# Another order of the steps in the three attention loops of a two-block kernel: scores, outputs, transposes, other work

## The reference

```python
for l in range(2):
    x  = ffn(x);  xc = ffn(xc)
    u  = mod_norm(x) @ w_in[l];  uc = mod_norm(xc) @ w_in[l]
    if l == 0:      # the context tokens are used as keys alone in the last layer
        yc = concat(conv(uc), pool(uc), softmax(qc kc' / 8) vc) @ w_out[l]
        xc = ffn(xc + gate * yc)
    # latent queries in blocks of 128: 8 rows x 16 columns; their keys are a band of
    # 32 columns in each of 8 rows (256 keys, bias from a table, masked) and 256 context keys
    y = concat(conv(u), pool(u), softmax([q k_near' / 8 + bias, q kc' / 8]) [v_near, vc]) @ w_out[l]
    x = ffn(x + gate * y)
```

## Time and profile before

| | |
|---|---|
| time, median of 3 runs | 3379.51 us (3378.93 to 3380.56) |
| profiled execution | 3378.85 us, of which the span of the trace is 3377.0 us |
| TensorE (matmuls) busy | 3265.8 us, 97% |
| VectorE busy | 2493.1 us, 74% |
| ScalarE busy | 1275.4 us, 38% |
| context loop in the trace | 1438 to 1503.4 us |
| first latent loop | 1548.3 to 1643.3 us |
| second latent loop | 2837.1 to about 2960 us |

### The profile page before, as it was taken

How to read it: one execution, slowest core, us unless ns; L and a number is a source line. 1 busy time by engine, 2 the same in 40 slices (tenths; PEclk the granted TensorE clock), 3 DMA queues, 4 the chain that set the end, 5 groups by cost and what they waited for, 6 DMA issues and landing times. The chain is left out here.

```text
span 3377.0 us, 45852 instructions
## 1 busy us (share of the span) xinstructions
PE 3265.8 (97%) x18042; PEld 2901.4 (86%) x18042; DVE 2493.1 (74%) x4610; ACT 1275.4 (38%) x2257; POOL 628.6 (19%) x657
## 2 busy tenths in 40 slices
PE   7989999999999999999999999999999999999998
PEld 6788778888999998978899999989999978788887
DVE  5576578888888997576788889888999865653333
ACT  4475542333323234334533333443332343432222
POOL 0100011112422220301052222142222212000000
PEclk9999999999999999999999999999999999999999
DMA  5201245564233333522113333323333343123332
GB/s 168 63 26 51 80 159 184 172 187 135 74 110 118 117 91 113 149 88 81 60 57 111 117 113 106 97 72 103 103 111 118 94 128 87 38 81 98 96 99 77
DMA packets 381929, 348.90 MB, mean 103 GB/s; under 512 B 17440, under 2 KB 338336, under 8 KB 381200
## 3 DMA queue, kind: packets, MB, share of 16 engines
q1 hardware_dynamic: 337696, 250.74, 24.5%
q0 software_dynamic: 17232, 46.84, 4.7%
q10 hardware_dynamic: 26784, 48.37, 4.6%
HBM read 339.60 MB, written 2.10 MB: 101 GB/s over the span
## 5 line engine op out<-in xcount | busy, mean ns | idle before, releaser
L816 PE MATMUL ps<-Hh,hib 128*128 128x512 f32 (+2 forms) x2672 | 956.2, 358 | 14.2 <-DVE Hl L2508 6.4
L816 PE MATMUL ps<-Hl,hib 128*128 128x512 f32 (+2 forms) x2672 | 947.0, 354 | 0.0
L816 PE MATMUL ps<-Hh,lob 128*128 128x512 f32 (+2 forms) x2672 | 946.4, 354 | 0.0
L1604 ACT ACTIVATE hib<-rawb 128x1024 fp32r<-128x1024 f32 (+2 forms) x589 | 508.3, 872 | 573.6 <-PE ps L816 570.7
L2376 DVE TENSOR_TENSOR lob<-rawb,hib 128x1024 fp32r<-128x1024 f32 (+2 forms) x361 | 441.0, 1225 | 384.6 <-ACT hib L1604 382.5
L816 PEld LDWEIGHTS ps<-Hh,hib 128*128 128x128 f32 x2672 | 507.9, 190 | 77.9 <-DVE Hl L2508 12.1
L816 PEld LDWEIGHTS ps<-Hh,lob 128*128 128x128 f32 x2672 | 507.8, 190 | 52.6
L816 PEld LDWEIGHTS ps<-Hl,hib 128*128 128x128 f32 x2672 | 508.4, 190 | 49.2 <-issue 0.5
L816 PE MATMUL ps<-Gha,hib 128*128 128x512 f32 (+1 forms) x704 | 238.6, 339 | 4.8 <-DVE lob L2376 3.4
L816 PE MATMUL ps<-Gla,hib 128*128 128x512 f32 (+1 forms) x704 | 237.3, 337 | 0.0
L816 PE MATMUL ps<-Gha,lob 128*128 128x512 f32 (+1 forms) x704 | 236.6, 336 | 0.0
(11 more groups left out here) (329 smaller groups left out, 5863.8 us busy)
## 6 DMA issues: line engine op xcount, KB each, us to landing
rawb<-in_ffn_w_in SPq DMA_DIRECT2D x114, 512.0 KB, 3.8
rawb<-in_ffn_w_out SPq DMA_DIRECT2D x76, 512.0 KB, 3.4
rawb<-in_w_in SPq DMA_DIRECT2D x74, 512.0 KB, 3.7
rawb<-in_w_ff SPq DMA_DIRECT2D x64, 512.0 KB, 3.6
rawb<-in_ffn_w_in SPq DMA_DIRECT2D x124, 256.0 KB, 3.3
MRa<-in_w_mod_t ACTq DMA_DIRECT2D x117, 256.0 KB, 3.1
MR<-in_w_mod_t POOLq DMA_DIRECT2D x112, 256.0 KB, 3.4
MRb<-in_w_mod_t ACTq DMA_DIRECT2D x59, 256.0 KB, 3.1
```

The source lines that it names most:

```text
L816: return e.matmul(out, lhsT, rhs, start=start, stop=stop)
L1604: return e.activation(out, src, f, **k)
```

## The change

TensorE's order in the latent and context loops goes from *transposes(step-d), scores(step), other work, outputs(step-d), bank of outputs(step-d-1) back* to *scores(step), outputs(step-d-1), their bank back at once, transposes(step-d), other work*, with d = `depth(s)`. The outputs of a pair are so issued one step later than before. ScalarE's order goes from *copies of the transposes(step-d), exponentials(step), other work, high half of the outputs(step-d-1)* to *high half of the outputs(step-d-1), copies(step-d), exponentials(step), other work*. VectorE's order stays. The number of steps, which was taken from the last entry of the skew list, is now an argument with the same value. No instruction is added or taken away.

```diff
-def by_pairs(number, stages, skew, beside, beside_do):
+def by_pairs(number, stages, skew, beside, beside_do, last):
 
-    for step in range(number + skew[-1]):
+    for step in range(number + last):
...
 (TensorE)
-                by_pairs(len(pairs), [n_turn, n_scores, "beside", n_out, n_final],
-                         [depth(s), 0, 0, depth(s), depth(s) + 1], beside_pairs(l, s), beside_do)
+                by_pairs(len(pairs), [n_scores, n_out, n_final, n_turn, "beside"],
+                         [0, depth(s) + 1, depth(s) + 1, depth(s), 0], beside_pairs(l, s), beside_do, depth(s) + 1)
...
 (ScalarE)
-                by_pairs(len(pairs), [n_turn, n_scores, "beside", n_final], [depth(s), 0, 0, depth(s) + 1], beside_pairs(l, s), beside_do)
+                by_pairs(len(pairs), [n_final, n_turn, n_scores, "beside"], [depth(s) + 1, depth(s), 0, 0], beside_pairs(l, s), beside_do,
+                         depth(s) + 1)
...
 (VectorE)
-                by_pairs(len(pairs), [n_scores, n_scale, "beside", n_final], [0, 1, 0, depth(s) + 1], beside_pairs(l, s), beside_do)
+                by_pairs(len(pairs), [n_scores, n_scale, "beside", n_final], [0, 1, 0, depth(s) + 1], beside_pairs(l, s), beside_do,
+                         depth(s) + 1)
```

## The result

| | before | after |
|---|---|---|
| time, median of 4 runs | 3380.03 us (3378.93 to 3380.56) | 3397.64 us (3395.78 to 3401.09) |
| span of the profiled execution | 3377.0 us | 3394.9 us |
| context loop, first scores to last outputs | 64.53 us | 74.06 us |
| first latent loop | 93.47 us | 95.85 us |
| second latent loop | 121.55 us | 127.78 us |

The change makes the kernel slower: by 17.6 us between the medians, which is 0.52%; the ratio on record is 1.0059 (95% interval 1.0046 to 1.0072). The loops' lengths are read on TensorE's timeline, from the start of the first row of scores to the start of the last row of outputs. They grew by 9.53 + 2.38 + 6.23 = 18.1 us, where the span grew by 17.9. The two other differences are −3.3 us ahead of the context loop and +3.0 between the latent loops, where both kernels issue the same instructions (more on this at the end).

A forecast was written before the change was run, and what follows sets the result against it. TensorE, busy 97% of the span, was taken to bound the kernel. Added waits of 8.7 (context), 2.5 (first latent) and 5.5 us (second latent) plus 6.8 for the clock gave 23.5, so 3403 us, range 3388 to 3414.

The forecast's parts named there:

- Transposes(2) for final(0): Context loop, step 4: transposes wait for VectorE's `n_final` of step 0, which frees the outputs' bank; +0.9 us.
- Outputs(3) for final(2): Context loop, step 6: outputs wait for VectorE's `n_final` of step 2, where nobody waited before; +1.4 us.
- Scores(7) for final(3): Context loop, step 7: scores wait 7.2 us for VectorE's `n_final` of step 3, behind convolution stage 1; +6.4 us.
- Scores(11) for exponentials(10): First latent loop, where tiles end: scores wait 2.1 us for a bank ScalarE's exponentials free, before 0.29; +1.8 us.
- Edge waits: First latent loop, steps with a tile: banks come free about when a 7.0 us step needs them; 0.3 us in all.
- Scores(9): Second latent loop: scores wait 4.3 us for VectorE's `n_final` of step 4, where it was 0.85; +3.4 us.
- The start: Second latent loop: transposes(0) instead of scores(3) wait for exponentials(2), saving 0.7 of the 2.67 us wait.
- The clock: TensorE's clock drops behind waits: 2.4 us each for two long ones, 1.0 each for two of 2.1; +6.8 us.
- The rule of the Trainium skill: Rival: short frequent waits in tile-less latent steps make TensorE alternate to half clock; some +15 us, 3418; 4 in 100.
- 1.84 did nothing: Argument against the half-clock rival: around the second latent loop's 1.84 us wait the clock stayed at 1.00.
- no work is added: Step in the sum: the change adds no work, and dense products behind the loops take nothing back.
- The faster rival: If VectorE's `n_final` of steps 3 and 4 is never waited for: up to 7.6 us gained, 3372 to 3377; 6 in 100.

The follow-up runs named there:

- experiment 1: Kernel before, with TensorE's and ScalarE's new order in the context loop only, old order in both latent loops: 3389.51 us, ratio 1.0033.
- experiment 2: Changed kernel with ScalarE's old order, so only TensorE's order is new: 3399.34 us, ratio 1.0062.
- experiment 4: Changed kernel, but in layer 0 (context and first latent loop) the outputs' bank returns to the list a step later: 3399.13 us, ratio 1.0059.
- experiment 5: Changed kernel with VectorE's `n_final` (low half of the outputs) ahead of its "beside" work: 3371.29 us, ratio 0.9981.
- experiment 8: New order with VectorE's early low half, and on ScalarE exponentials ahead of the copies: 3381.02 us, ratio 1.0010.
- experiment 3: Changed kernel with TensorE's old order, so only ScalarE's order is new: 3378.37 us, ratio 1.0001.
- experiment 6: Kernel before, with only VectorE's low half of the outputs moved ahead of its other work: 3381.33 us, ratio 1.0009.
- experiment 7: New order with VectorE's early low half in the context and second latent loops, first latent loop as before: 3372.68 us, ratio 0.9985.

## Why the prediction came out

The sign, the place and the releaser of each main wait came out as predicted, but for the start of the second latent loop; the time was 5 to 6 us too high, by a term that the sum lacked. Of the signs listed, one was just missed: the long wait was to be 6 to 8 us and was 5.94. Two small readings in the sum were off without consequence: final(4) ended at 2904.81 and not 2904.73, and 2903.7 less 2899.5 is 4.2, not 4.3.

**Waits.** Sums of TensorE's waits in the three loops, from its timeline:

| | before | after | more | predicted |
|---|---|---|---|---|
| context loop | 2.81 us | 10.41 us | +7.6 | +8.7 |
| first latent loop | 3.87 | 6.18 | +2.3 | +2.5 |
| second latent loop | 5.96 | 12.17 | +6.2 | +5.5 |

- *Context loop.* Transposes(2) for final(0): 1.43 in place of 0.52, +0.9 as predicted. Outputs(3) for final(2): 1.57, predicted 1.4. Scores(7) for final(3): 5.94, predicted 7.2; where the clock held ahead of it, in experiments 1 and 2, 7.40 and 7.39. From the low half's start to the end of final(3) were 10.21 us (1484.91 to 1495.12), predicted 10.2. Experiments 4 (bank's turn) and 5 (VectorE's order) remove these waits in different ways, which confirms the mechanism.
- *First latent loop.* Scores(11) for exponentials(10): 1.72, predicted 2.1. Edge waits: 0.51 in one place, 0.3 charged. Drain: 0.78, 0.78, 0.69 and 0.69 in place of 1.18, 0.69 and 0.69, the +0.4 predicted.
- *Second latent loop.* Outputs(2): 1.34, predicted 1.5. Scores(9): 3.80, predicted 4.3. Scores(13) and (15): 1.72 and 1.74, predicted 2.1 and 1.65. The start was wrong: instead of 2.0 in one wait there came 1.59, 0.64 and 0.56, together 2.8, so no part of the 2.67 was saved.

**The clock.** Predicted +6.8, measured +6.6, but by errors that cancel. From the windows, stretches at half clock with work under them: 1.7 us behind 1481, 1.9 behind the long wait, 1.7 behind 1617.86, 3.0 behind 2913.11, 1.7 behind 2942.10, together 10.0; and before 3.4 at the start of the second latent loop that are gone (the 1.7 at the start of the first are in both). I had charged 2.4 for each of the two long waits and 1.0 for each of the two of 2.1; the drop behind 1481 and the one saved at 2853 were in no term. The long wait's own stretch of half clock was 6.8 us long (1492 to 1500, at 0.54 and 0.61) and cost 1.9, since nearly half of it lay under the wait itself. The rule of the Trainium skill ("TensorE: Matmul & The Clock Gate", A second HAM failure mode) that I had made a rival did not come true here: in the steps without a tile, where it should have shown, the window from 1622 to 1626 is at 1.00, and each latent loop has one drop there, of 1.7 us, behind its wait of 1.72. In experiment 8, where four such steps in a row wait 0.5 to 0.6 us, the clock is 1.00 from 1602 to 1640. The argument held against that rival, "1.84 did nothing", was luck, though: in experiments 1, 3 and 6 a drop came behind the same wait of 1.84 us.

**The missing term.** Waits +16.1 and clock +6.6 give 22.7, and the loops got 18.1 longer. The 4.6 us between are in the steps that nothing holds up. I had taken a step's length as 6.97 in either order, as if only the waits could differ. The changed kernel shows (timeline of TensorE, starts of the masks of three successive steps, and the matmul of the tile before the second):

```profile
1584.65 0.39 PE L816 MATMUL ps<-near_maskr,identr 128*128 128x256 f32 x2
...
1591.19 0.39 PE L816 MATMUL ps<-Hh,lob 128*128 128x512 f32 x1
1591.42 0.44 PE L816 MATMUL ps<-near_maskr,identr 128*128 128x256 f32 x2
...
1598.24 0.39 PE L816 MATMUL ps<-near_maskr,identr 128*128 128x256 f32 x2
```

Steps of 6.77 and 6.82. The masks follow the last matmul of a tile after 0.23 us, at the tile's own pace. In the old order the outputs stood there and followed after 0.32 (timeline of TensorE, kernel before; the outputs start at 1592.48):

```profile
1592.16 0.39 PE L816 MATMUL ps<-Hh,lob 128*128 128x512 f32 x1
```

And in the old order the masks followed fp32 transposes. The context loop has no masks, and its steps are shorter too, by 0.21 us (outputs to outputs 7.43 before, 1458.30 to 1465.73, and 7.22 in experiment 5, 1457.26 to 1464.48). There the saving sits behind the transposes: scores followed their start after 0.58 us (timeline of the kernel before, the first of the two pieces below; the scores at 1474.90 are in the earlier trace rows), a tile follows it after 0.41 (that of experiment 5, the second piece):

```profile
1474.32 0.65 PE L819 MATMUL ps<-con,near_P 128*128 128x128 f32 x4
```

```profile
1472.30 0.66 PE L819 MATMUL ps<-con,near_P 128*128 128x128 f32 x4
1472.71 0.47 PE L816 MATMUL ps<-Hh,hib 128*128 128x512 f32 x1
```

28 steps in the three loops have a tile among their scores (8, 8 and 12): at 0.17 us they make 4.8, near the 4.6 that are missing. By loops the agreement is looser: 1.7, 1.6 and 1.3 us are missing, where 0.17 a step gives 1.4, 1.4 and 2.0. The term is in every trace of the new order, not in this one alone. What is left of a loop, from its first matmul of scores to its last of outputs, without TensorE's waits and without what half clock cost:

| | TensorE in the old order | TensorE in the new order |
|---|---|---|
| context loop | 61.9 to 62.1 us (before, experiments 3, 6) | 60.4 to 61.2 (changed, 1, 2, 4, 5, 7, 8) |
| first latent loop | 89.2 to 89.5 (before, 1, 3, 6, 7) | 87.6 to 88.7 (changed, 2, 4, 5, 8) |
| second latent loop | 113.3 to 113.7 (before, 1, 3, 6) | 111.6 to 112.3 (changed, 2, 4, 5, 7, 8) |

The two orders never overlap, and experiments 2 and 3 stand on different sides: it is TensorE's order that makes the work shorter, not ScalarE's. Which pair of neighbours saves how much is read from single starts; the kernel that would isolate it was not tried. In the prediction it is the step "no work is added", read as "the same work takes the same time in any order".

**The faster rival** needed final(3) and final(4) never to be waited for. Experiment 5 made that so, by another way than the one I gave it, and came out at 3371.29 where the rival stood at 3372 to 3377. Its price list was off in the parts. The loops of experiment 5 are 6.0 us shorter than before: TensorE's waits in them are 1.2 us more (the 2.67 did not go, it came in three pieces of 2.8 together), half clock costs 3.4 less, and the shorter steps give the other 3.8. So the place in that range is in part luck.

**From profile to remedy.** The Trainium skill ("Perfetto Trace Analysis", Optimization Strategy) says to find the gaps of the limiting engine, the instruction that ends each, and to make that one start sooner. Experiment 5 against experiment 4 agrees: moving the releaser gave 26 us; moving the bank's turn in the list, in layer 0, gave 8.9 us in one loop and took 9.4 in the next. The same section lets gaps that repeat stand for too few buffers; here the costly gaps came once each, where a long piece of VectorE's work (stage 1) fell ahead of the release.

## What to carry to other kernels

When an order is changed on one engine, write out which buffer each step gets and who frees it, and then ask where in its own step the freeing instruction stands: 0.28 us of VectorE behind 10 us of other work cost more than the new order gained, and one line on VectorE turned +17.6 us into −7.5. Judge a reordering together with the order of the engine that frees its buffers, not alone: each of the two edits by itself gave nothing or a loss, and both together gave 7 us. And time an undisturbed step in both orders before taking its length as given.

## What the runs showed of the hardware that was not expected

- The same wait may or may not bring the half clock. The wait of 1.01 or 1.02 us for line 3189 at the start of the first latent loop was followed by a granted clock of 0.57 over four us in the changed kernel (1560 to 1564) and 0.61 before (1554 to 1558), and by 1.00 in experiment 5 (1550 to 1556); a drop came behind it in five of the ten traces. Behind the 2.67 us of the old order a drop came in all four traces that have it, behind the 1.59 us that stand there in the new order in two of six (experiments 2 and 7). Waits of 1.72 us for `near_P` brought it at 1617.86 and 2942.10 in the changed kernel; in experiment 5 one did and the one at 2921.54 did not. Around 1481 a wait of 1.57 brought it in one kernel and not in another with the same instructions on TensorE. A drop cost 1.7 or 3.4 us in all of these, less what lay under a wait.
- So single executions differ by whole drops: the context loop began between 1433.5 and 1438.7 us in kernels that are identical up to there. Ahead of it the trace has 41.0 us at half clock in the kernel before and 30.7 in the changed one, which began it 3.3 us sooner; between the latent loops 17.1 and 23.9, and the changed kernel took 3.0 us longer there. TensorE's idle time is the same in both stretches to 0.1 us. A term of 2 us can be read in a loop's length, not in one execution's span.
- The same matmuls in another order take another time: a step of a latent loop with a tile is 6.97 us long when the tile stands between scores and outputs, and 6.79 when it stands between the fp32 transposes and the masks; a step of the context loop is 7.43 and 7.22.
